# Attention: the modulation tile of an odd pair stands behind the turned probabilities, not in front of them

## What is computed

```python
mod = (c_act @ w_ada[layer] + b_ada[layer])[:, None, :]
shift1, scale1, gate1, shift2, scale2, gate2 = jnp.split(mod, 6, axis=-1)
hn = modulate(rms_norm(h, norm1_g[layer]), shift1, scale1)
proj = hn @ w_in[layer]
...
for window, dilation in DILATED_PATTERNS:
    o, l = dilated_window_attention(qa, ka, va, table_a, window, dilation)
...
p1 = jax.nn.softmax(jnp.einsum('bhqd,bhkd->bhqk', q1b, k1) * scale + bias, axis=-1)
p2 = jax.nn.softmax(jnp.einsum('bhqd,bhkd->bhqk', q2b, k2) * scale + bias, axis=-1)
return jnp.einsum('bhqk,bhkd->bhqd', p1 - lam * p2, v)
...
mixed = jnp.concatenate([o_a, o_b], axis=-1) @ w_out[layer]
h = h + gate1 * mixed
hn = modulate(rms_norm(h, norm2_g[layer]), shift2, scale2)
```

## Time and profile before

| | |
|---|---|
| median of 3 runs | 1588.24 us (1587.87 to 1588.24) |
| the profiled execution | 1589.81 us, span 1588.0 us |
| PE busy | 1235.2 us (78%) |
| DVE busy | 451.4 us (28%) |
| ACT busy | 222.6 us (14%) |
| POOL busy | 150.9 us (10%) |
| moved by DMA | 542.93 MB, mean 342 GB/s |
| the chain that ended last, by engine | PE 49%, DMA 40% |

### The profile page before, as it was taken

How to read it: one execution, slowest core, us unless ns; L and a number is a source line. 1 busy time by engine, 2 the same in 40 slices (tenths; PEclk the granted TensorE clock), 3 DMA queues, 4 the chain that set the end, 5 groups by cost and what they waited for, 6 DMA issues and landing times.

```text
span 1588.0 us, 17761 instructions
## 1 busy us (share of the span) xinstructions
PE 1235.2 (78%) x7570; PEld 691.3 (44%) x7570; DVE 451.4 (28%) x902; ACT 222.6 (14%) x458; POOL 150.9 (10%) x151
## 2 busy tenths in 40 slices
PE   7999999999999999987665566666566566656565
PEld 3876679998888888831111111111111111111111
DVE  4567756774533568220000000000000000000001
ACT  2324522232113231020000000000000000000001
POOL 1110056641100031000000000000000000000000
PEclk9999999999999999999787877787886887797878
DMA  9986476458944335799999999999999999999997
GB/s 387 342 264 248 168 291 213 160 175 335 394 155 159 106 114 209 296 364 429 428 428 429 428 428 429 428 428 428 428 429 428 428 428 429 428 428 429 427 429 304
DMA packets 52310, 542.93 MB, mean 342 GB/s; under 512 B 5932, under 2 KB 7980, under 8 KB 13196
## 3 DMA queue, kind: packets, MB, share of 16 engines
q1 hardware_dynamic: 45564, 511.03, 78.8%
q0 software_dynamic: 4352, 26.82, 4.3%
q10 hardware_dynamic: 2320, 3.98, 0.9%
HBM read 539.97 MB, written 1.84 MB: 341 GB/s over the span
## 4 chain that ended last, share of the span: by engine, by line
PE 49%; DMA 40%; another core or an unknown queue 4%; DVE 3%; ACT 1%; SPq 1%; issue 1%; ACTq 0%; DVEq 0%
DMA arena<-in_exp_w_dram 19%; DMA ring<-in_exp_w_dram 15%; PE L L1987 8%; PE L L2152 7%; DMA tok<-in_exp_w_dram 6%; PE X L2371 5%; PE L L2099 5%; PE X L2399 4%; PE L L1821 4%; PE X L2046 3%; PE L L1832 2%; PE L L2271 2%; PE L L1972 2%; PE X L2201 1%
## 5 line engine op out<-in xcount | busy, mean ns | idle before, releaser
L2371 PE MATMUL X<-arena,side 128*32 128x512 f32 x1280 | 194.6, 738 | 114.8 <-DMA arena<-in_exp_w_dram 114.8
L2371 PEld LDWEIGHTS X<-arena,side 128*32 128x32 f32 x1280 | 39.8, 123 | 268.5 <-DMA arena<-in_exp_w_dram 193.8
L1651 DVE TENSOR_TENSOR side<-side,X 128x512 f32<-128x512 f32 x16 | 11.0, 688 | 497.7 <-ACT side L998 497.7
L2371 PE MATMUL X<-ring,side 128*32 128x512 f32 x512 | 86.4, 808 | 71.1 <-DMA ring<-in_exp_w_dram 71.1
L2399 PE MATMUL X<-ring,side 128*32 128x512 f32 x512 | 81.4, 767 | 46.7 <-DMA ring<-in_exp_w_dram 46.4
L2152 PE MATMUL L<-tok,ring 128*128 128x256 f32 x448 | 99.4, 379 | 0.3 <-ACT tok L834 0.3
L665 POOL TENSOR_TENSOR side<-side 128x256 f32<-128x256 f32 x16 | 9.9, 616 | 869.5 <-DVE side L1661 806.7
L1656 DVE TENSOR_TENSOR side<-X,side 128x512 f32<-128x512 f32 x16 | 11.1, 692 | 281.5 <-PE X L2399 281.5
L2152 PEld LDWEIGHTS L<-tok,ring 128*128 128x128 f32 x448 | 84.3, 190 | 13.9 <-issue 3.1
L998 ACT ACTIVATE side<-X 128x512 f32<-128x512 f32 x16 | 9.6, 597 | 514.1 <-PE X L2371 514.1
L2099 PE MATMUL L<-arena,ring 128*128 128x256 f32 x352 | 77.4, 379 | 0.3 <-DVE arena L1391 0.3
(11 more groups left out here) (406 smaller groups left out, 1669.3 us busy)
## 6 DMA issues: line engine op xcount, KB each, us to landing
arena<-in_exp_w_dram SPq DMA_DIRECT2D x96, 2048.0 KB, 50.2
ring<-in_exp_w_dram SPq DMA_DIRECT2D x64, 2048.0 KB, 49.9
ring<-in_w_in_dram SPq DMA_DIRECT2D x34, 1024.0 KB, 5.2
more<-in_exp_w_dram SPq DMA_DIRECT2D x15, 2048.0 KB, 50.2
tok<-in_exp_w_dram SPq DMA_DIRECT2D x15, 2048.0 KB, 49.7
ring<-in_w_up_dram SPq DMA_DIRECT2D x22, 1024.0 KB, 4.9
ring<-in_w_ada_dram SPq DMA_DIRECT2D x16, 1024.0 KB, 9.5
arena<-in_ada_w_dram POOLq DMA_DIRECT2D x15, 1024.0 KB, 10.0
```

What stands on the lines that cost most here:

```text
L2371: last = MM(X[CAP * j:CAP * j + CAP, w, :], xe[:, k % 2, k // 2, :], v, start=(k == 0), stop=(k == KT - 1))
```

## The change

In steps 3, 5, 7, 9, 11 and 13 the modulation tile is written behind the turn of the pair, not ahead of it. The tile in step 0 keeps its place.

```diff
                 if p == 0:
                     mod_columns(1)
                     mod_products(17)
-                elif p % 2 and p < 14 and p > 1:
-                    mod_products(17 + p // 2)
                 if p in (14, 16):
                     keep_busy(X[:, 0, T:T + P], 4)
                 if p < 16:
                     turn_probs(p)
+                if p % 2 and p < 14 and p > 1:
+                    mod_products(17 + p // 2)
                 if p >= 1:
                     pv(p - 1)
```

## The result

With the tile behind the turn the kernel takes 1591.13 us (median of 13 runs, 1590.13 to 1591.85) against 1588.24 us (median of 13, 1586.71 to 1589.59): the ratio is 1.0018, with a 95% interval of 1.0010 to 1.0026. It is slower, by 2.9 us and by less than the 0.2% named ahead; 1590.4 us had been forecast. The profiled execution took 1591.36 us for a span of 1589.6 us, 1.6 us more than the span of before.

What follows compares the result with a forecast made beforehand. PE was taken to bound the attention with very little slack, DVE and ACT close behind. First half 0.1 us plus 2.1 us from steps 9, 11 and 13 gave +2.2 on the median 1588.24: 1590.4 us, range 1588.9 to 1591.9.

Steps and rivals of the forecast that it cites:

- The chain hands everything on: From the projection's start at 179.26 us, any attention delay reaches the expert-weight stream and the end in full.
- The first half costs 0.1 us: Steps 3, 5 and 7: turn inputs are ready in time, so the swap costs +0.1 us (bounds 0 and +0.2).
- Step 9, +0.99: The turn of pair 9 waits uncovered for ACT's scaling, then the tile runs; pv(8) comes 0.99 us later.
- Step 10 takes up the idle 0.56 us, and the delay goes on over DVE and ACT: Idle time before pair 10's turn absorbs all but 0.4 us; pair 12's exponential still moves by +0.85 us.
- Step 11, +1.48, and step 13, +2.25: Later scalings of pairs 11 and 13 plus the tile: pv(10) 1.48 us later, pv(12) 2.25 us later.
- The tail over DVE's copy and the inverse of pair 15: DVE copies pv(12)'s result before inverting pair 15, so inverse, last turn and projection start move by about 2.1 us.
- The idle time: about 3.3 us uncovered, 1.24 us gone: Seen from PE: 3.3 us of waits exposed in steps 9, 11, 13; 1.24 us idle before turns 10, 12, 14 disappears.
- The weight load that might be done ahead: The tile's first weight load might run during the exposed wait, saving 0.07 us per step: 2.0 instead of 2.2; not taken off.
- Slack of PE: Rival: PE's own idle time takes up the wait at no cost, 1588.2 + 0 to 0.5 us; chance 0.08.
- Faster: Rival: earlier turns win at most PE's idle time before turns 10, 12, 14, 15, 1.4 us: 1586.8 us; chance 0.03.
- The clock: Rival: new PE gaps drop TensorE to half clock at the attention's end, +3.7 us on top, 1594 us; chance 0.03.
- More than the sum from the first half: Rival: DVE's inverse falls behind in steps 5 and 7, +3.2 to +5 us, 1591.4 to 1593 us; chance 0.08.

Runs made afterwards that it cites:

- first_half: Kernel before with only the tiles of steps 3, 5 and 7 behind the turn: first scores to projection 40.03 us against 39.90; whole kernel 0.9999.
- only_nine: Kernel before with only the tile of step 9 behind the turn: first scores to projection 40.84 us against 39.90.
- second_half: Kernel before with only the tiles of steps 9, 11 and 13 behind the turn: first scores to projection 42.46 us against 39.90; whole kernel 1.0032.
- filled: Changed kernel plus eight turns of the identity ahead of the turns of pairs 9, 11 and 13: first scores to projection 42.58 us, changed kernel 42.58.

## Why the prediction was right

It was right in sign, in mechanism and in its range; its size was 0.5 us short of the ruler (2.2 against 2.68) and 0.7 us short of the medians (2.2 against 2.9).

- *The chain hands everything on.* Right in what it gave: 422.14 us on both sides, and the same span of the stream within its scatter. Its place was wrong. The prediction let the hand-over last to 718 to 728 us and said that nothing in this stretch is paid back; in the profile of after PE lost another 1.7 us at 708 us, and that did not reach the end. What carries the loss on is when SP's loads start, from 601.40 (603.48) us on and before PE's work at 708 us.
- *The first half costs 0.1 us.* Right: `first_half` +0.13.
- *Step 9, +0.99.* Right in kind. By the time from the first scores, pv(8) went from 25.34 to 26.55 us, +1.21, with 0.12 of it from the first half, so +1.09.
- *Step 10 takes up the idle 0.56 us, and the delay goes on over DVE and ACT.* Right, the exponential of pair 12 waits 0.87 us for its maximum; `only_nine` shows it alone.
- *Step 11, +1.48, and step 13, +2.25.* pv(10) from 30.04 to 31.86, +1.82, and pv(12) from 34.39 to 37.18, +2.79. With the 0.12 of the first half the sum said 1.6 and 2.4. The mis-sized term is the tile itself, "0.99" in each step. It starts 0.36 us behind the turn (163.95 to 164.31), where the product with the values stood 0.28 us behind it (164.42 to 164.70 in the earlier trace rows): 0.1 us in each of three steps. And behind a tile pv(10) and pv(12) take longer up to what follows them: 0.65 us (170.62 to 171.27) against 0.54, and 0.55 (175.94 to 176.49) against 0.44: 0.1 us each. The point on the weight load below has the reason. Together 0.5 us, the whole of what was missing.
- *The tail over DVE's copy and the inverse of pair 15.* Right; the idle time before the turn of pair 15 grew from 0.17 to 0.61 us, which I had not named among the signs. In the sum seen from PE it is what was left out: 3.33 - 1.24 + 0.44 + 0.13 = 2.66 us.
- *The idle time: about 3.3 us uncovered, 1.24 us gone.* 1.01 + 1.16 + 1.16 = 3.33 us, and none is left before pairs 10, 12 and 14.
- *The weight load that might be done ahead.* The rule of the Trainium skill (page "TensorE: Matmul & The Clock Gate", section "Architectural detail") would have made the sum smaller; the tile's first load was not done ahead. PE's weight loads in after, at step 9 and for pv(10):

```profile
163.94 0.20 PEld L1910 LDWEIGHTS L<-sq,arena 128*128 128x128 f32 x2 [1.41 <-ACT arena L806]
164.31 0.16 PEld L1762 LDWEIGHTS L<-ring,arena 128*32 128x32 f32 x8 [0.17 <-issue]
...
170.62 0.52 PEld L1922 LDWEIGHTS L<-arena 128*128 128x128 f32 x4 [0.84 <-issue]
```

  And before, for the tile of step 9 and for pv(10):

```profile
163.34 0.16 PEld L1762 LDWEIGHTS L<-ring,arena 128*32 128x32 f32 x8 [0.33 <-issue]
...
169.30 0.53 PEld L1922 LDWEIGHTS L<-arena 128*128 128x128 f32 x4
```

  The load path was idle for 1.41 us, and the tile's first load still came behind those of the turn that waited. The wait need not be what held it back: before, where no instruction with a wait for the scaling stands ahead of it, the tile's load comes no earlier than its product either, both at 163.34. What the rows show is that a load goes ahead where the weights keep their shape: pv(10) stood behind a turn, both 128 x 128, and its load started at 169.30 for a product at 169.40, which agrees with the rule. Behind the tile of 128 x 32 weights load and product both start at 170.62. That is the 0.1 us by which pv(10) takes longer; for pv(12) the rows are alike. No run has a load of the same shape behind one that waits.

- *The rivals.* Slack of PE: refuted by `only_nine` and `second_half`. Faster: refuted. The clock: 1.00 through the gaps, and `filled` shows that they are free; the gap between two PE instructions that the prediction leaned on, in 674 to 690 us of before, was at most 1.09 us, those here are up to 1.16. More than the sum from the first half: refuted by `first_half`.

## What to carry to other kernels

Work that waits for nothing belongs in front of an instruction that has to wait, not behind it. In front it was free here up to the length of the wait; behind, three tiles of 0.99 us cost 2.56 us, because what the engine feeds came later and led back to the next wait. An engine's idle time elsewhere takes up little of a delay that travels over other engines (0.99 us became 0.94 in `only_nine`), so follow it to the next wait before booking the slack. Where whole times scatter, measure from one instruction of a stage to the first of the next.

## What the runs showed of the hardware

- Four float32 products of 128 x 32 weights with 128 x 512, each into its own strip of 32 rows of one bank, take 0.99 us together; one of them alone takes 0.98. With 128 columns the four take 0.36 us, not a quarter.
- The load of weights of 128 x 128 behind a turn of the same shape started 0.10 us ahead of its product (169.30, 169.40, before); behind a tile with weights of 128 x 32 it started with it (170.62, after).
- A transposition of two tiles is followed by a product with 128 x 128 weights after 0.28 us, and by one with 128 x 32 weights after 0.36 us, although it waits for nothing that the profile shows. The Trainium skill, page "TensorEngine Tiling (Array Packing)", section "Key Properties", says that a change of the tiling mode drains TensorE; the 0.08 us would agree with that, and no run here took it apart.
- From the end of an instruction on ACT to the start of the turn on PE that it releases it is 0.04 to 0.06 us.
